# A transformer block pair on one core: a third product bank in the retention stage, top-k counts placed ahead of its steps on DVE, a pair's turn one slot later, and a reordered hand-over where the gated projection ends

## The reference, cut to what matters

```
# end of the first block
ple_gate = sigmoid(rmsnorm(x, g_ple) @ w_ple_gate)
x = x + ple_gate * (p @ w_ple_proj)

# second block
h = rmsnorm_2(x, norm1_w);  z = h @ w_in
qa, c_kv, iq, ik, iw, qb, kb, vb, gb = split(z)
score = sum_h iw_h * relu(iq_h . ik)           # masked; top 256 keys of each row are kept
out_a = softmax(qa . ka over the kept keys) @ va
# retention, 8 heads, chunks of the sequence
scores = (qc @ kc^T) * inner_decay
y = scores @ vc + (qc @ state) * query_decay
state = state * chunk_decay + (kc * key_decay)^T @ vc
y = groupnorm(y) * ret_gn_w + ret_gn_b         # mean and variance of each token and head
out_b = silu(gb) * y
x = x + concat(out_a, out_b) @ w_out
```

## Time and profile before

| | us |
|---|---|
| median of 3 runs | 2835.56 |
| lowest, highest | 2830.56, 2840.65 |
| the profiled execution | 2836.64 |
| its span, first to last instruction | 2835.3 |
| busy: PE, DVE, POOL, ACT | 2703.3, 1371.1, 1169.6, 953.5 |

### The profile page before, as it was taken

The page is one execution under the profiler, slowest core; times in us unless marked ns, Lnnn a source line. Parts: engine busy times, 40 slices in busy tenths (PEclk is TensorE's granted clock), DMA queues, the critical chain, the costliest instruction groups (busy, mean ns, idle before and its releaser), DMA issues.

```text
span 2835.3 us, 35101 instructions
## 1 busy us (share of the span) xinstructions
PE 2703.3 (95%) x12720; PEld 2191.4 (77%) x12720; DVE 1371.1 (48%) x2655; ACT 953.5 (34%) x1776; POOL 1169.6 (41%) x826
## 2 busy tenths in 40 slices
PE   7999999998999999999898898987999999999999
PEld 6877677777888888887766676766887888888887
DVE  4114344447666662235448777757725433333222
ACT  5333333333333332233352222345523433333210
POOL 2110011454666665444313233125435666666542
PEclk9999999999999999999999999889999999999999
DMA  3110101411222244211211000121131222226221
GB/s 131 35 48 31 38 30 63 153 67 67 75 82 90 82 144 176 75 54 62 87 53 56 27 34 30 45 75 42 35 141 67 80 85 82 90 74 232 95 67 67
DMA packets 78315, 217.48 MB, mean 77 GB/s; under 512 B 7968, under 2 KB 20544, under 8 KB 77760
## 3 DMA queue, kind: packets, MB, share of 16 engines
q1 hardware_dynamic: 78144, 215.23, 21.2%
HBM read 168.01 MB, written 47.19 MB: 76 GB/s over the span
## 4 chain that ended last, share of the span: by engine, by line
PE 86%; DVE 7%; issue 3%; ACT 2%; POOL 1%; DMA 1%; SPq 0%; DVEq 0%; ACTq 0%; POOLq 0%
PE PS L863 9%; PE PS L864 9%; PE PS L865 9%; PE PS L622 8%; PE PS L624 8%; PE PS L623 8%; PE PS L881 5%; PE PS L882 5%; PE PS L883 5%; PE PS L733 3%; PE PS L744 3%; PE PS L1144 2%; DVE acc L1819 1%; PE PS L723 1%; PE PS L1125 1%
## 5 line engine op out<-in xcount | busy, mean ns | idle before, releaser
L622 PE MATMUL PS<-Hh,Wl 128*128 128x512 f32 x1072 | 446.8, 417 | 43.3 <-DVE K L1915 15.3
L2827 POOL TENSOR_TENSOR Wl<-Wr,Wh 128x1024 fp32r<-128x1024 f32 (+1 forms) x79 | 178.6, 2263 | 666.2 <-ACT Wh L2087 666.2
L624 PE MATMUL PS<-Hh,Wh 128*128 128x512 f32 x1072 | 429.3, 400 | 0.0
L623 PE MATMUL PS<-Hl,Wh 128*128 128x512 f32 x1072 | 428.2, 399 | 0.0
L2887 POOL TENSOR_TENSOR RG<-RW,RG 128x512 fp32r<-128x512 f32 x176 | 243.9, 1390 | 144.5 <-ACT RG L2323 144.4
L1613 DVE TENSOR_TENSOR XA<-PS,XA 128x512 f32<-128x512 f32 x192 | 132.5, 691 | 332.9 <-PE PS L883 332.9
L622 PEld LDWEIGHTS PS<-Hh,Wl 128*128 128x128 f32 x1072 | 210.0, 196 | 96.9 <-DVE K L1915 21.9
L881 PE MATMUL PS<-Hh,RG 128*128 128x512 f32 x704 | 275.0, 391 | 0.7 <-issue 0.4
L882 PE MATMUL PS<-Hl,RG 128*128 128x512 f32 x704 | 274.4, 390 | 0.0
L883 PE MATMUL PS<-Hh,RG 128*128 128x512 f32 x704 | 274.3, 390 | 0.0
L863 PE MATMUL PS<-Hh,RG 128*128 128x512 f32 x640 | 249.2, 389 | 0.0
(11 more groups left out here) (337 smaller groups left out, 5114.3 us busy)
## 6 DMA issues: line engine op xcount, KB each, us to landing
RW<-in_wg SPq DMA_DIRECT2D x44, 512.0 KB, 3.5
RW<-in_wu SPq DMA_DIRECT2D x44, 512.0 KB, 4.5
R<-in_wd SPq DMA_DIRECT2D x88, 256.0 KB, 3.0
hgscr<-GB SPq DMA_DIRECT2D x44, 512.0 KB, 2.6
G<-hgscr SPq DMA_DIRECT2D x40, 512.0 KB, 6.7
Wr<-in_wi SPq DMA_DIRECT2D x23, 512.0 KB, 3.3
Wr<-in_wo SPq DMA_DIRECT2D x16, 512.0 KB, 3.3
spill<-X SPq DMA_DIRECT2D x16, 512.0 KB, 2.6
```

Source lines behind the costliest of these rows:

```text
L622: pe.matmul(ps(b), k.Wl[:, s, wc], xh[:, kx, sl], start=kk == 0, stop=False)
L623: pe.matmul(ps(b), k.Wh[:, s, wc], xl[:, kx, sl], start=False, stop=False)
L624: i = pe.matmul(ps(b), k.Wh[:, s, wc], xh[:, kx, sl], start=False, stop=kk == nk - 1)
L2827: pool.tensor_tensor(k.Wl[:, s, 0:w], k.Wr[:, s, 0:w], k.Wh[:, s, 0:w].bitcast(F32), ALU.subtract).then_inc(*up("w_lo", "w_lo", u))
```

## The change

At the hand-over DVE no longer adds a square right after each projection of tiles 6 and 7: it empties and adds x for all four, then makes Hl of tiles 6 and 7 of half 0, adds the two squares of tile 6, makes three Hl of half 1, and adds the two squares of tile 7. ACT makes Hh of tiles 6 and 7 ahead of the square of (7,0). `stat` of half 0 moves from piece 3 to piece 5 of the first product, `spread` of half 0 from piece 7 of it to piece 1 of the next, and the work behind them with it. In the retention stage the products rotate through banks 0, 1, 2; before the `qa` products the rotation is (0, 1) again. On DVE a tick advances the counts twice and then the retention step. The 16 scalings are split over two ticks, and PE's turn of YT, ACT's gain, DVE's gate and SP's store move back: the turn by one tick, from 18 to 19, gate and store by two.

```diff
 (PE)
-    product([(ui, H, ("iq", 0), False)], 8, 0, {3: lambda: stat("n1", 0), 7: lambda: spread("n1", 0)}, fresh=lo("n1"))
-    product([(uw, H, ("iw", 0), False)], 8, 0, {2: lambda: stat("n1", 1), 6: lambda: spread("n1", 1)})
+    product([(ui, H, ("iq", 0), False)], 8, 0, {5: lambda: stat("n1", 0)}, fresh=lo("n1"))
+    product([(uw, H, ("iw", 0), False)], 8, 0, {1: lambda: spread("n1", 0), 2: lambda: stat("n1", 1), 6: lambda: spread("n1", 1)})
...
 (PE retention, ahead of rt_normed)
-        yield
+        for _ in range(2):
+            yield
...
 (PE, DVE and ACT, ahead of the pairs, and ahead of qa)
+    bank.of, bank.n = (0, 1, 2), 0
...
+    bank.of, bank.n = (0, 1), 0
...
 (DVE)
     def tick():
-        bg.tick()
         bg2.tick()
         bg2.tick()
+        bg.tick()
...
 (DVE projected)
-        if m >= 6:
-            add("n1", m, half, k.sq_no["n1", half, m])
...
+    def n1_add(m):
+        for half in range(2):
+            add("n1", m, half, k.sq_no["n1", half, m])
+
     for m in (6, 7):
         n1_low(m, 0)
-    for m in range(4):
+    n1_add(6)
+    for m in range(3):
         n1_low(m, 1)
-    walk(8, 3, {3: lambda: n1_root(0)}, tick)
-    for m in range(4, 8):
+    n1_add(7)
+    walk(8, 3, {5: lambda: n1_root(0)}, tick)
+    for m in range(3, 8):
         n1_low(m, 1)
...
 (DVE retention)
         for c in range(8):
+            if c == 4:
+                yield
...
         i.then_inc(*up("ret_v", "rt_normed", j))
-        yield
+        for _ in range(2):
+            yield
...
 (ACT)
-            square("n1", m, half, k.XA[:, m, half_of(half)], [("x", "n1", m, half)])
             if (m, half) == (7, 0):
                 n1_high(6, 0)
                 n1_high(7, 0)
+            square("n1", m, half, k.XA[:, m, half_of(half)], [("x", "n1", m, half)])
...
-    walk(8, 3, {3: lambda: root("n1", 0)}, tick)
+    walk(8, 3, {5: lambda: root("n1", 0)}, tick)
     for m in range(4, 8):
         n1_high(m, 1)
-    row1(0)
     iq_high(0)
     use(1)
-    walk(8, 3, {2: lambda: root("n1", 1), 6: lambda: row1(1)}, tick)
+    walk(8, 3, {1: lambda: row1(0), 2: lambda: root("n1", 1), 6: lambda: row1(1)}, tick)
...
 (ACT retention, after the root)
-        yield
+        for _ in range(2):
+            yield
...
 (SP retention)
-        for _ in range(17):
+        for _ in range(19):
             yield
```

## The result

The changed kernel takes 2816.85 us (median of 5 runs, 2814.81 to 2819.47), the kernel before 2831.51 beside it: ratio 0.9943, 95% interval 0.9923 to 0.9964. That is faster by 0.57%, where 1.3% was forecast. The waits for the banks went as the sum says, and most of what else it counted on was lost to waits that are new.

The account below looks back on a forecast made before the run. PE was taken to bound the kernel, losing time in waits and half-clock stretches. The terms summed to -36.8 us, from 2836.64 to 2799.8, so a median of 2799; range 2786 to 2818.

Parts of the forecast that it names:

- line 1915: Retention pairs: with three banks PE no longer waits for DVE to empty a rotation's bank, minus 15.3 us.
- line 2727: After v in the pairs: g's first product takes the third bank, so PE's wait for ACT's emptying goes, minus 3.4 us.
- turn, pairs 0 to 2, with the wait for v's copy: PE's turn of YT: waits 1.4 us plus 0.8 for v's copy instead of about 3.4, minus 3.3 in all.
- turn, pair 3: Last pair's turn of YT: counts nearly used up and hn work between, so its 2.3 us wait goes.
- clock in the pairs: Half-clock stretches in the pairs: of 18.6 us lost, all but three short stretches given back, minus 13.8; bounds minus 18.6 and 7.
- clock in `qa`: The `qa` products: two more half-clock stretches lose about half of what they cost, minus 2.6 us.
- statistic's emptying: In `qa`, PE's wait for a DVE operation that now follows its step directly shrinks, minus 1.0 us.
- DVE's lag: Pair passages: two counts ahead of a pair's first step make masks late, 0.9 at three, 1.0 after pair 0, plus 3.6.
- hand-over: Into the first product: PE restarts earlier but waits for half 0's statistic, plus 1.3 us; bounds minus 8 and plus 2.5.
- The prediction's own row on POOL holding DVE: Hand-over: line 1185, reading two SBUF tiles, took 2.40 us beside POOL's Wl, 0.69 otherwise.
- The "up to 2" for POOL's subtractions: DVE's lag at pair passages: POOL's subtractions can add up to 2 us to the 13.6 of 14 steps and gate.
- DVE becomes the bound: Rival for the pairs: masks late at passages, turn keeps its old wait, some clock lost, 2816 us; chance 0.13.

Follow-up runs that it names:

- the kernel with all three edits: Changed kernel plus tile 7's adds ahead of half 1's Hl, POOL's g-weight subtraction held until YT is normed, one count a tick in g products: 2794.27 us, ratio 0.9854.
- POOL's wait alone: Changed kernel with POOL's weight subtraction at unit g held until the scalings of the pair before are done: 2813.26 us, ratio 0.9932.
- fewer counts alone: Changed kernel with one counting step a tick, not two, in g's second product (both in pair 0), made up later in `qa`: 2814.82 us, ratio 0.9941.
- the early adds: Changed kernel with both adds of tile 7 ahead of the three Hl of half 1 on DVE: 2812.09 us, ratio 0.9925.
- the kernel with POOL's wait and fewer counts: Changed kernel with POOL held ahead of g's weights and one counting step a tick in g's products, adds as changed: 2803.67 us, ratio 0.9892.

## Why the prediction was too fast

The forecast of 2799 was 17.9 us too low; beside the kernel before, which measured 2831.51 this time, the change gave 14.7 us for 36.8, so it fell 22.1 short. The sum by its own terms, and what each came to in the trace:

| term | forecast | measured |
|---|---|---|
| line 1915 | -15.3 | -15.3 |
| line 2727 | -3.4 | -3.4 |
| turn, pairs 0 to 2, with the wait for v's copy | -3.3 | +3.5 |
| turn, pair 3 | -2.3 | -2.3 |
| clock in the pairs | -13.8 | -10.1 |
| clock in `qa` | -2.6 | about -1.8 |
| statistic's emptying | -1.0 | -1.6 |
| DVE's lag | +3.6 | +11.1 |
| hand-over | +1.3 | +2.6, interval -0.6 to +6 |

Turn: 11.4 + 3.1 now against 10.2 + 0.8. The statistic's row joins two waits of `qa`, 1.2 to 0.3 and 1.6 to 0.9. The hand-over's is the ratio of that edit alone. The rows sum to -17.3; the two medians lie 14.7 apart, the two profiled spans 21.1, so 2.6 or 3.8 us belong to no row. The prediction's own four parts of DVE's lag (three times 0.9, and 1.0) come to 3.7, not 3.6, which changes nothing. In size the largest miss is DVE's lag (7.5 us), then the turn (6.8), then the clock (4.5 in pairs and `qa`).

**The step that failed first is the turn, minus 3.3.** "Eight scalings (1.83)", counted twice, was taken from the kernel before, where POOL was idle at that time, and the moved turn was not followed through ACT's order: its gain of K stood ahead of Wh before, and no longer does. The prediction's own row on POOL holding DVE (2.40 for 0.69 us) priced the effect, and I applied it at the hand-over alone. Three holds of some 2.1 us make most of the 6.8 us. That POOL is the cause is shown by the kernel in which it waits: 1.87 us for 3.99, and 5.1 for 11.4 us at the turns.

The Trainium skill, SBUF — State Buffer, section Who interferes with whom, counts `tensor_scalar` among the operations that can take the port pair shared with GpSimd, except in the form that also writes out its accumulator. By it the scalings and two of the four small operations (1841, 1817) can be held and the counts are not. The rows agree: 3.99 for 1.88 us, 2.22 for 0.17, and the 1024-wide count took 1.28 us at 1618.89, with POOL idle, and 1.28 at 1580.81, when POOL was busy from 1580.57 to 1581.85. The other two (1843, 1819) have two SBUF inputs, as line 1185 in the prediction, and the rows show them held too (2.29 us).

**The second is DVE's lag, plus 3.6.** Its largest part is where pair 0 ends, taken at 1.0 us and measured at 4.55. The reasoning had the cause right (DVE counts without rest from 1507) and mis-sized it: all that PE gains in pair 0 brings it nearer to a DVE that gains nothing, and DVE had had 2.90 us in hand. The rest, 6.5 us, lies in masks and updates. The three largest of these waits (2.22, 1.54 and 1.57 us) stand behind small operations held by POOL: 2.22 and 2.29 us, 2.35 and 2.28, 1.47 and 1.21. The "up to 2" for POOL's subtractions understated that, since POOL's other operations (3067, 3048) hold DVE too. In the changed pairs DVE is busy for 66.4 of 75 us and 68.4 of 76, where the earlier trace rows had 61.9 of 82. I had put the lag down to the two counts ahead of a pair's first step. The runs bear that out at one place only: the wait at the start of pair 1 is 4.55 us with the new tick, 3.07 with the banks alone and 1.63 with the old tick in the changed kernel. Over the stage the masks are as late with the old tick (11.7 us at line 1034 with the banks alone, 8.8 and 7.3 in the changed kernel with old and new tick), so the order of the tick is not the main cause.

**The clock** followed: in the pairs one stretch more than forecast, after the 4.55 us, and one longer; in `qa` one where no wait stands (below). That small waits do it no harm was right where they came: in the kernel with all three edits the clock stays at 1.00 past waits of 0.78 and 1.60 us with eight transposes behind each. The rule on transposes from the Trainium skill (TensorE: Matmul & The Clock Gate, Part 4: PE-mode transpose), by which such a stretch should still fall to the lower level, is not borne out by these rows. The page speaks of the engine's transpose mode, and the trace names these instructions only as MATMUL, so whether they are in that mode stays open.

**What was right**: the third bank and the waits that it removes; the hand-over's chain, with 2.5 and 6.0 us for "about 2.5" and "6 to 7". The last pair's turn lost its 2.3 us as forecast, but not for being moved: it waits nothing with the old turn and the new tick, 3.1 us with the new turn and the old tick, and 4.2 in each kernel with the later turn that puts counts off to `qa`. So it goes with how far the counts have got.

The outcome is the rival "DVE becomes the bound", priced at 2816. Its mechanism is met in its two parts, masks late and the turn keeping its wait. That its price fits within 1 us is in part luck: its terms were 4.4, 5.7 and 7 us for 7.5, 6.8 and 4.5 measured, and it was reckoned from a kernel before that measured 4 us more. But DVE is no bound by amount. POOL's wait alone took 6.3 us from the turn and put 4.3 at the masks; fewer counts alone took 7.4 us from masks and updates and put 3.7 at the turn. With both, neither came back but for the 4.2 us in `qa`; the clock was 1.00, 0.98 and 0.98 in the three pairs, and 1.00 in all with the early adds too, while DVE was still busy for 62.7 of 70 us. It was late at certain places, by order and by POOL's holds, and each repair exposed the next place.

Open: whether the early adds are worth more in company. They gave 4.8 us alone, 6.7 with fewer counts and 9.4 with POOL's wait as well (by the ratios 5, 10 and 11), while their waits changed alike (line 638 from 6.0 to 0.2 or 0.4, with 1.4 new at 648). Each ratio's interval is some 4 us to either side, so the three may be one value. Nor was POOL's wait tried with the old turn.

## What to carry to other kernels

When one engine's step is moved in a fixed order, follow what stood behind it on every other engine: here a later turn freed ACT, ACT freed POOL, and POOL landed on the eight operations that the turn waits for. Where a helper engine is near 90% busy in step with the main one, removing one wait can expose the next, and repairs tried one at a time can look worth little; combine them before judging. And price a known hold (here POOL's operations on DVE's) at every place where the two engines can now meet, small operations too.

## What the runs showed of the hardware

An operation on 128x6 numbers in SBUF lasts until POOL's operation beside it ends: 2.22 and 2.29 us for 0.17, and 0.97 where it began 0.95 us before that end (1582.35 to 1583.32, POOL's to 1583.29). A count, which reads 128x1024 and accumulates, kept its 1.28 us beside POOL.

A wait of 2.2 us of PE does not always lower its clock. The changed kernel waited 2.22 us at 1589.31 and the window after it has 1.00; the kernel with all three edits waited as long at 1723.24 and stays at 1.00; the kernel with POOL's wait and fewer counts waited 2.20 us at 1725.44, and the clock fell:

```profile
1724.00:1728.00 4.00, 2.56 (x7) 2.08 (x8) 3.80 (x15) 0.52 (x2) 1.43 (x2) 0.63 0.41 131
```

In the kernel before, all six waits of 1.8 to 2.2 us inside pairs 1 to 3 were followed by half clock.

And the clock fell where PE had hardly waited at all. Windows over the `qa` products of the changed kernel:

```profile
1809.00:1813.00 4.00, 3.74 (x27) 3.07 (x26) 2.57 (x8) 2.22 (x5) 0.00 (x0) 1.00 0.01 4
1813.00:1817.00 4.00, 4.00 (x14) 3.13 (x13) 1.39 (x4) 0.00 (x0) 0.00 (x0) 0.53 0.00 0
```

What PE did ahead of it beside the large products were the retention's matmuls of 64 columns and 16 of two columns for a statistic:

```profile
1809.93 0.95 PE L657 MATMUL PS<-mats,K 128*128 128x2 f32 x8
1811.14 1.05 PE L657 MATMUL PS<-mats,K 128*128 128x2 f32 x8 [0.26 <-DVE sml L1229]
```

So my reading that each half-clock stretch is the consequence of a wait holds for the pairs of the kernel before, and not everywhere. No run here tells what in this stretch lowered it.
